# The state-space layer of a two-layer decoder trunk in chunks of four steps

## The reference, cut to what matters

```python
    lam_bar = jnp.exp(lam * dt)
    b_bar = ((lam_bar - 1.0) / lam)[..., None] * b
    bu = jnp.einsum('bsgh,gph->bsgp', uf.astype(jnp.complex64), b_bar)
    a = jnp.broadcast_to(lam_bar, (1, seq, SSM_GROUPS, SSM_STATE))
...
    _, states = lax.associative_scan(combine, (a, bu), axis=1)
    c = lax.complex(c_re.astype(f32), c_im.astype(f32))
    y = jnp.real(jnp.einsum('bsgp,ghp->bsgh', states, c))
    y = y + d.astype(f32).reshape(SSM_GROUPS, SSM_GROUP_CH) * uf
    y = jax.nn.gelu(y.reshape(bsz, seq, SSM_WIDTH)).astype(u.dtype)
    return y * jax.nn.sigmoid(y @ w_glu + b_glu)
```

## Time and profile before

| | us |
|---|---|
| median of 3 runs | 1784.97 (1784.24 to 1786.6) |
| profiled execution, its own time | 1786.59 |
| its span, first to last instruction | 1784.4 |
| mean granted TensorE clock | 0.969 |
| TensorE busy | 1673.2 |
| VectorE busy | 1390.6 |
| ScalarE busy | 884.8 |
| GpSimd busy | 221.1 |

### The profile page before, as it was taken

The page is one execution under the profiler, slowest core; times in us unless marked ns, Lnnn a source line. Parts: engine busy times, 40 slices in busy tenths (PEclk is TensorE's granted clock), DMA queues, the critical chain, the costliest instruction groups (busy, mean ns, idle before and its releaser), DMA issues.

```text
span 1784.4 us, 22506 instructions
## 1 busy us (share of the span) xinstructions
PE 1673.2 (94%) x8124; PEld 1352.1 (76%) x8124; DVE 1390.6 (78%) x1328; ACT 884.8 (50%) x731; POOL 221.1 (12%) x386
## 2 busy tenths in 40 slices
PE   7778999999797899899999999999999999999995
PEld 5556858999675685678878888888788788788784
DVE  8887356555557834599889899899898898998896
ACT  1011123443200121367767677676777776777672
POOL 5381009400028200000000000000000000000000
PEclk9888999999898899999999999999999999999998
DMA  8422266555332225589999999999899999999991
GB/s 281 149 75 91 71 235 208 200 188 188 97 115 72 71 95 177 201 289 378 346 338 372 340 341 367 334 346 373 319 369 342 341 363 353 343 365 342 337 379 62
DMA packets 217706, 457.37 MB, mean 256 GB/s; under 512 B 7910, under 2 KB 60167, under 8 KB 216888
## 3 DMA queue, kind: packets, MB, share of 16 engines
q1 hardware_dynamic: 216888, 451.96, 71.7%
q0 software_dynamic: 768, 4.75, 0.7%
HBM read 454.06 MB, written 2.62 MB: 256 GB/s over the span
## 4 chain that ended last, share of the span: by engine, by line
PE 82%; DVE 13%; issue 3%; ACT 1%; POOL 0%; DVEq 0%; DMA 0%; SPq 0%; POOLq 0%; ACTq 0%
PE psum L501 18%; PE psum L503 18%; PE psum L502 18%; PE psum L546 6%; PE psum L689 3%; PE psum L703 3%; PE psum L508 2%; PE psum L510 2%; PE psum L509 2%; PE psum L843 2%; DVE arena L1409 1%; DVE wl L319 1%; PE psum L862 1%; ACT wh L314 1%; PE psum L588 1%
## 5 line engine op out<-in xcount | busy, mean ns | idle before, releaser
L319 DVE TENSOR_TENSOR wl<-ring,wh 128x2048 fp32r<-128x2048 f32 x379 | 863.6, 2297 | 174.6 <-ACT wh L314 170.8
L314 ACT ACTIVATE wh<-ring 128x2048 fp32r<-128x2048 f32 x379 | 728.1, 1923 | 218.1 <-PE psum L503 149.6
L501 PE MATMUL psum<-wh,xgh 128*128 128x512 f32 x896 | 356.3, 398 | 7.5 <-DVE wl L319 6.1
L503 PE MATMUL psum<-wh,xgl 128*128 128x512 f32 x896 | 349.8, 390 | 0.0
L502 PE MATMUL psum<-wl,xgh 128*128 128x512 f32 x896 | 349.0, 389 | 0.0
L546 PE MATMUL psum<-xT,ring 128*128 128x256 f32 (+1 forms) x896 | 210.0, 402 | 12.2 <-DMA ring<-in_w_in 11.5
L501 PE MATMUL psum<-wh,hidh 128*128 128x512 f32 x536 | 210.2, 392 | 3.8 <-DVE hidl L1606 2.1
L546 PEld LDWEIGHTS psum<-xT,ring 128*128 128x128 f32 (+1 forms) x896 | 169.6, 194 | 53.6 <-issue 23.1
L503 PE MATMUL psum<-wh,hidl 128*128 128x512 f32 x536 | 209.4, 391 | 0.0
L502 PE MATMUL psum<-wl,hidh 128*128 128x512 f32 x536 | 209.2, 390 | 0.0
L501 PEld LDWEIGHTS psum<-wh,xgh 128*128 128x128 f32 x896 | 168.2, 188 | 46.9 <-DVE wl L319 9.4
(11 more groups left out here) (260 smaller groups left out, 1750.5 us busy)
## 6 DMA issues: line engine op xcount, KB each, us to landing
ring<-in_moe_gu SPq DMA_DIRECT2D x224, 1024.0 KB, 7.2
ring<-in_moe_dn SPq DMA_DIRECT2D x112, 1024.0 KB, 6.9
ring<-in_w_in SPq DMA_DIRECT2D x26, 1024.0 KB, 5.4
ring<-in_w_gu SPq DMA_DIRECT2D x22, 1024.0 KB, 5.1
ring<-in_w_dn SPq DMA_DIRECT2D x11, 1024.0 KB, 4.9
ring<-in_w_out SPq DMA_DIRECT2D x8, 1024.0 KB, 5.1
ring<-in_w_pg SPq DMA_DIRECT2D x8, 1024.0 KB, 4.9
lnp<-in_ln POOLq DMA_DIRECT2D x4, 1024.0 KB, 7.4
```

The source lines that it names most:

```text
L314: eng.activation(wh[:, u % SPLIT, :], ring[:, u % RING, :], ACT.Copy).then_inc(hi_ready, 1)
L319: eng.tensor_tensor(wl[:, u % SPLIT, :], ring[:, u % RING, :], wh[:, u % SPLIT, :].bitcast(F32), ALU.subtract).then_inc(lo_ready, 1)
L501: pe.matmul(dst, ah, bh, start=first, stop=False, skip_group_check=True)
L503: return pe.matmul(dst, al, bh, start=False, stop=last, skip_group_check=True)
```

## The change

The recurrence is cut into 64 chunks of four steps (`CL` = 4, `NC` = 64). The input maps are widened: for each pair a 128x128 map (`gin`) takes the inputs of four steps (4 x 32 channels, laid out in the tile `shifted`) to the state after the chunk. The scan then runs over 64 chunks and all 16 pairs in two calls of `scan_states`. Back to the steps, the output is the sum of two parts: the state at the end of the chunk before, through one map for each of the four steps (`cpow`), and the inputs inside the chunk, through a `local` map.

The maps are made on the chip in each layer. VectorE multiplies the raw maps with the powers of `lambda_bar` (`input_powers` into `bpow`, `output_powers` into `cpow` and `c0`), TensorE turns `bpow` around (`turn_maps`) and multiplies it with `c0` (`local_maps`), ScalarE copies both out of PSUM. ScalarE (three quarters) and GpSimd (one) write `shifted`. `bpow`, `cpow` and `c0` are zero outside the blocks that VectorE writes, so GpSimd sets them to zero first (`zero_maps`), once for each layer. They lie in `arena`, over `wh` and `wl`, so the second time GpSimd waits for the last split unit of the dense channel mixer. Angle tables are 64 chunks long, one for each layer (`make_turns`).

```diff
 TensorE
+                def turn_maps():
+                    pe.wait_ge(bpow_ready, l + 1)
...
+                    for n in range(8):
+                        if n >= 4:
+                            pe.wait_ge(gin_ready, 8 * l + n - 3)
...
+                                mm = pe.transpose(b[:, (2 * t + ri) * P:(2 * t + ri + 1) * P],
+                                                  bpow[:, ri, 2 * n + t].rearrange("p k c -> p (k c)"), ident)
+                        mm.then_inc(gin_full, 1)
+                def local_maps():
+                    pe.wait_ge(cpow_ready, l + 1)
+                    pe.wait_ge(gin_ready, 8 * (l + 1))
+                    for i in range(ST):
+                        for ri in range(2):
+                            mm = pe.matmul(bank[7][:, i * 32:(i + 1) * 32], bpow[:, ri, i]..., c0[:, ri, i], ...)
+                    mm.then_inc(local_full, 1)
                 def input_states(b):
+                    if b:
+                        pe.wait_ge(bu_free, n)
+                    for i in range(8):
...
                         for ri in range(2):
-                            mm = pe.matmul(bank[2 + t][:, ri * SEQ:(ri + 1) * SEQ], bmat[q:q + 32, l, ri, c, :],
-                                           uT[q:q + 32, c, :], start=True, stop=True)
+                            mm = pe.matmul(bank[2 + ri][:, i * NC:(i + 1) * NC], gin[:, 8 * b + i, ri, :], u4[:, :, CL - 1],
+                                           start=True, stop=True)
                 def output_states(b):
+                    pe.wait_ge(local_ready, l + 1)
+                    pe.wait_ge(xs_ready, n + 1)
+                    for cc in range(2):
+                        for q in range(4):
+                            pe.matmul(y[32 * q:32 * q + 32, cc * SEQ:(cc + 1) * SEQ], local[:, 8 * b + i], shifted[:, 8 * b + i], ...)
+                        for t in range(CL):
+                            for ri in range(2):
+                                for q in range(4):
+                                    mm = pe.matmul(y5[32 * q:32 * q + 32, cc, 1:NC, t], cpow[:, ri, 8 * b + i, t], x[:, ri, i, 0:NC - 1], ...)
                     mm.then_inc(y_full, 1)
+                project("q")
+                turn_maps()
+                project("q")
                 input_states(0)
-                project("q")
-                input_states(1)
...
                 project("kv")
-                input_states(3), output_states(1), scores(0)
+                local_maps(), input_states(1), scores(0)
                 project("g")
-                input_states(4), output_states(2)
+                output_states(0)
                 project("g")
-                transpose_probs(0), input_states(5), output_states(3)
+                transpose_probs(0), output_states(1)
                 project("g")
-                attend(0), scores(1), input_states(6), output_states(4)
+                attend(0), scores(1)
                 project("g")
-                transpose_probs(1), input_states(7), output_states(5)
+                transpose_probs(1)
 ScalarE
+                    shift_inputs(lambda d, s: act.activation(d, s, ACT.Copy), g, (0, 1, 2), shifted_ready[0])
...
+                        for n in range(8):
+                            act.wait_ge(gin_full, 8 * l + n + 1)
+                            act.activation(dst, bank[4 + n % 4][:, :], ACT.Copy).then_inc(gin_ready, 1)
 GpSimd
-            make_phases(0, 1)
+            zero_maps()
+            zero(shifted.rearrange("p a n -> p (a n)"))
+            pool.wait_ge(powers_ready, 1)
+            make_turns(0)
...
                     root(0)
                     load_ln(1)
+                    make_turns(1)
                     split_used(pool, PLAIN_UNITS)
                     pool.dma_start(pT[:], pT_in[1]...)
-                    make_phases(1, 0), make_phases(1, 1)
+                    split_used(pool, DENSE_UNITS + FFN_UNITS - 1)
+                    zero_maps()
                     root(1)
 VectorE
+            input_powers(0)
             (the rest of the parameters)
             for l in range(DEPTH):
+                if l:
+                    input_powers(l)
+                output_powers(l)
                 def scan_states(b):
+                    if b == 0:
+                        dve.wait_ge(turns_ready, l + 1)
+                        dve.wait_ge(local_full, l + 1)
...
-                    for t in range(2):
+                    for i in range(8):
                         for ri in range(2):
-                            ins = dve.tensor_tensor_scan(vw[:, 2 + ri, t * SEQ:(t + 1) * SEQ], ...)
+                            ins = dve.tensor_tensor_scan(vw[:, 2 + ri, i * NC:(i + 1) * NC], ...)
-                scan_states(4, between=0), skip_term(1), scan_states(5), logits(1)
-                scan_states(6, between=1), skip_term(2), scan_states(7), logits(2), normalise(2), skip_term(3)
+                scan_states(0), scan_states(1), logits(0), skip_terms(0), normalise(0), skip_terms(1)
                 (the GELU)
+                logits(1), normalise(1), logits(2), normalise(2)
                 logits(3), normalise(3)
```

More of the change, by code:

```diff
@@ L103, in program @@
         cst = place("cst", [P, 4 * P + 8])
-        small = place("small", [P, 40, 32])
+        small = place("small", [P, 48, 32])
         pT = place("pT", [P, 2, SEQ])
@@ L578, in output_states @@
[L578 to L589 removed]
+                    n = 2 * l + b
@@ L1203, in _ @@
             for l in range(DEPTH):
-                for b in range(8):
-                    if not vector_states(b):
-                        states(pool, l, b)
-                    if b % 2 and b // 2 + 2 < 4:
-                        make_phases(l, b // 2 + 2)
+                for g in range(2):
+                    pool.wait_ge(u_ready, 2 * l + g + 1)
+                    shift_inputs(pool.tensor_copy, g, (3,), shifted_ready[1])
                 pool.wait_ge(pT_lo, l + 1)
```

373 lines of the change are left out of this document (215 added, 158 removed).

## The result

The changed kernel takes 1775.46 us (median of 5 runs, 1771.44 to 1776.92) beside 1784.97 (5 runs, 1784.23 to 1786.6) for the kernel before: the ratio is 0.9943, with a 95% interval of 0.9932 to 0.9955. The gain of 0.57% is more than the 0.2% that a measurement can tell from none. The profiled execution took 1776.07 us, its span is 1774.0.

A forecast was written before the change was run, and what follows sets the result against it. In the mixers VectorE sets the end and TensorE pays by waits and low clock; behind them TensorE bounds. First mixer -17.4, second -0.1, zeroing +5.6 give -11.9 us from 1784.97: 1773 us, range 1754 to 1792.

The forecast's parts named there:

- First mixer: First layer's mixer: second mixer's forecast plus 9.1 us for bias rows and low clock; 171.1 against 188.5, 17.4 us won.
- the copies into `shifted`: First mixer: ScalarE's 24 copies, at most 14.4 us, hidden beside two projections; GpSimd's eight come behind its angle table, unpriced.
- The 3.4 us for the clock behind the bias rows: First mixer: after the bias rows the clock runs at half speed for 6.9 us, costing 3.4 us.
- `output_states`: TensorE's products from states back to steps, two calls a layer: 0.04 us a record, 6.0 us a call, 12.0 together.
- Rival 1: Narrow output_states records cost 0.072 us whatever their width: +16.4 us, 1789.5, slower than before; chance 0.18.
- Second mixer: Second layer's mixer: 120.4 us kept, 33.6 added, 8.0 for the clock; 162.0 against 162.1, 0.1 us won.
- The two long waits: Second mixer: TensorE's waits for VectorE's `normalise`, 10.34 and 8.23 us, would go, 18.6 us.
- rival 4: Mixers' waits only move, because scans still cost 0.61 us each: some 10 us in each layer, 1793; chance 0.05.
- The clock: Clock falls at local_maps, slowing its end, the second input_states and next projection: 8.0 us a layer, from 0 to 12.
- rival 2: The clock doesn't fall around local_maps in the mixers: 16 us more won, 1757; chance 0.20.
- The zeroing: Between the layers GpSimd's memsets take 9.0 us ahead of the norm's root, delaying VectorE by 5.6 us (0 to 15.4).
- rival 3: Memsets between the layers cost as much as two-input products: 9.8 us more, 1783, no measurable change; chance 0.12.

The follow-up runs named there:

- shift_first: Changed kernel, with GpSimd making the four shifted copies of the first channel group before the first layer's rotations instead of behind them; 1760.5 us, ratio 0.9856.
- combined: Changed kernel with shift_first, ScalarE instead of GpSimd clearing the maps' buffers between the layers, and maps_between together; 1743.3 us, ratio 0.9761.
- combined_again: The same kernel as combined, timed a second time for comparison on one chip; 1738.4 us, ratio 0.9739.
- one_group: Changed kernel, with output_states' loop over the four column groups moved outermost, so eight narrow products in a row use the same 32 columns; 1790.1 us, ratio 1.0027.
- maps_early: Changed kernel, with local_maps ahead of the kv projection instead of behind it in both layers; 1767.8 us, ratio 0.9883.
- maps_between: Changed kernel, with local_maps in one stretch inside the kv projection, between k's and v's products; 1766.6 us, ratio 0.9908.

## Why the prediction was right, and where only its total was

The time is 2.5 us above the 1773 forecast. Behind that stand errors of 13 and of 17 us that met, so the total is this near by luck; the mechanism (waits gone, the clock's fall, the late norm) was right, with one wait missed.

**First mixer, 171.1 us forecast, 178.0 measured.** The step that failed is the one on the copies into `shifted`: "and hidden; GpSimd's eight come behind its angle table". The text saw the order of the queue and priced only ScalarE's side. No number was given for GpSimd's end, and it set the path: TensorE was through with the projection at 51.1 us, and the first four of GpSimd's copies let it go on at 62.4. That is 11.25 us of wait, 3.2 for `input_states(0)` (7.06 for 3.86) and 2.5 for k's products (14.09 for 11.61), 17.0 us. shift_first gave back 17.1 us in that mixer. ScalarE's copies were indeed hidden, and the powers were ready at 64.9 (forecast: 68 at the latest, needed at 74). The 3.4 us for the clock behind the bias rows did not come either: in the changed kernel the bias rows stand as before, and the projection behind the second four takes 7.17 us. In the kernel before, the products of 32 rows (L571) stood between, but they are not needed for a fall. combined has no L571, and its projection behind the first four bias rows is slow, at a granted clock of 0.81; in combined_again it is the one behind the second four, 8.86 us:

```profile
24.34 8.84 PE L539 MATMUL psum<-xT,ring 128*128 128x256 f32 x32
```

Of the thirteen profiles without L571 only these two, of one kernel, have it; why is open.

**`output_states`, 12.0 us a layer forecast, 5.5 measured.** A record was priced at 0.04 us, with 0.027 as the lower bound; it is 0.014. The step "half the weights and half the moving columns would make that 0.036" scaled a row on two column groups and gave nothing for going round four of them. one_group shows that this is where the factor lies. Over four calls 13.0 us were counted too many, which just pays for most of the missing wait. Rival 1, which had the loss, is out with it.

**Second mixer, 162.0 us forecast, 152.8 measured.** 6.5 of the 9.2 are `output_states`. The rest of the step list held: `turn_maps` 3.8 (4.0), `local_maps` with its clock 8.3 (8.9), the wait 3.2 (2.6), `input_states(1)` slower by 3.2 (3.5), the projection behind it by 1.6 (2.6), the transposes' wait 0.91 (1.0). The two long waits are gone. The sixteen scans of a call take 3.02 us (3.2), so rival 4 is out.

**The clock** fell where the forecast put it, and rival 2 is out. The reason given was "a stretch without one dense product". The runs are finer: a stretch of `local_maps` ends at or near 1.2 GHz in each place tried (granted 0.58 over its last 2.9 us in the changed kernel, 0.50 over the last 3.4 in maps_early and 3.5 in maps_between); woven among v's products it doesn't; and behind the wait `input_states(1)` is slow even so. It was at full clock in each kernel in which a projection's products stood between the two. But there the wait was gone as well, so the runs don't tell the dense products from the missing wait.

**The zeroing, 5.6 us forecast, 7.2 measured.** The memsets took 7.85 us (9.0 taken), 0.85 ns an element. That is far from rival 3's 18.7. The estimate from the Trainium skill, "GPSIMD Engine Reference", section on performance versus the Vector engine, was 7.9 us, and the trace agrees. But the step "whatever they take beyond 3.3 us is late" failed: it started both engines at the same product. VectorE's norm begins with the first token block, 2.7 us before the last product ends, so the memsets had 0.6 us of cover. Two errors that partly cancel: 9.0 less 3.4 was 5.6, and 7.85 less 0.6 is 7.2.

**Left open.** What decides between 1.2 and 2.4 GHz in these stretches was narrowed by place, not explained: `local_maps` behind the same products took 8.1 to 10.5 us in different layers and executions. What only the first layer has was priced short, too: its first projection takes 9.68 us (9.74 before) at a granted clock of 1.00 where the next takes 7.17, and no run asks why.

## What to carry to other kernels

When a step is given to a second engine, price that engine's queue to the moment of the last output as well, each instruction in it included; "it comes behind X" is a number that is still missing. Before pricing many small products, ask which part of the array each goes to: going round four column groups made them 3.4 times cheaper than staying in one, and mixing widths seems to have cost 0.15 us a change. Try few-column work between dense products, early enough that they cover the wait behind it.

## What the runs showed of the hardware that was not expected

- Narrow products (32 output partitions, 63 columns) cost 14 ns a record round four column groups, 48 ns in one.
- Three memsets in a row on GpSimd stopped VectorE's 128x1024 `tensor_scalar` for as long as they ran (8.31 us for 0.81), and its 64x256 copies (5.03 for 1.00 for four), while the small statistics beside another memset kept their 0.15 to 0.21 us.
- GpSimd's copies of 32 partitions took 0.51 us each alone and 1.2 beside VectorE's products with two inputs.
- A stream that alternates products of 64 and 128 columns kept the clock that it found, 0.50 for 51 us in one layer and 1.00 for 29 in the other.
